# The down matrices' requests, from SP to ACT, in the expert stage of a two-layer encoder

## What is computed

```python
DEPTH = 2; D_MODEL = 1024; N_EXPERTS = 32; TOP_K = 2; EXPERT_FF = 512
for i in range(DEPTH):
    ...                                     # conv, attention, gates, cross attention
    h = h + hier_moe(rmsnorm(h, norm_ffn_g[i]), ..., w1[i], w3[i], w2[i])

# inside hier_moe, for the tokens xb of expert e
hdn = jax.nn.silu(xb @ w1[e]) * (xb @ w3[e])      # up: 1024x512, twice
y = hdn @ w2[e]                                   # down: 512x1024
out = jnp.einsum('nkd,nk->nd', y, weights)
```

## Time and profile before

| | us |
|---|---|
| median of the runs | 1767.76 |
| lowest and highest of the runs | 1762.47 and 1770.13 |
| span of the profiled execution | 1763.5 |
| PE busy | 1498.1 (85%) |
| DVE busy | 616.6 (35%) |
| ACT busy | 528.7 (30%) |
| POOL busy | 57.3 (3%) |
| bytes moved by DMA | 530.92 MB, mean 301 GB/s |

### The profile page before, as it was taken

One profiled execution on the slowest core, in us unless ns is written; L12 is line 12 of the kernel. 1 busy time (PEld: TensorE's weight loads), 2 busy tenths in 40 slices (PEclk: granted clock), 3 DMA queues, 4 the chain that ended last, 5 costly groups with the idle time before them and its releaser, 6 DMA issues.

```text
span 1763.5 us, 24557 instructions
## 1 busy us (share of the span) xinstructions
PE 1498.1 (85%) x9704; PEld 1006.0 (57%) x9704; DVE 616.6 (35%) x1020; ACT 528.7 (30%) x829; POOL 57.3 (3%) x100
## 2 busy tenths in 40 slices
PE   8999999999886767676789999999998777776766
PEld 7788889886332323232277888998853232323322
DVE  5556777554110100000054668775530000000101
ACT  5436564543100000000153465645431000000001
POOL 3011000000000000000000200000000000000000
PEclk8999999999998888889899999999999989898988
DMA  8536335755999999999955462457469999999997
GB/s 232 191 120 215 127 113 191 286 191 217 405 422 422 422 421 422 422 422 422 415 181 187 126 203 97 144 193 285 162 280 423 422 422 422 422 422 422 422 422 306
DMA packets 118165, 530.92 MB, mean 301 GB/s; under 512 B 8808, under 2 KB 9000, under 8 KB 68934
## 3 DMA queue, kind: packets, MB, share of 16 engines
q1 hardware_dynamic: 114944, 524.13, 74.9%
q0 software_dynamic: 3136, 5.73, 1.6%
q10 hardware_dynamic: 12, 0.05, 0.0%
HBM read 524.63 MB, written 1.05 MB: 298 GB/s over the span
## 4 chain that ended last, share of the span: by engine, by line
PE 56%; DMA 36%; DVE 2%; SPq 2%; issue 2%; ACT 2%; PEldq 0%; DVEq 0%; ACTq 0%
DMA ring<-in_w_dram 35%; PE ps L2054 11%; PE ps L1670 7%; PE ps L1675 7%; PE ps L1671 7%; PE ps L1726 4%; PE ps L1727 4%; PE ps L1732 4%; SPq L561 2%; PE ps L1772 2%; PE ps L1695 1%; PE ps L1701 1%; PE ps L1696 1%; PE ps L1829 1%; PE ps L2023 1%
## 5 line engine op out<-in xcount | busy, mean ns | idle before, releaser
L2054 PE MATMUL ps<-ring,big 128*32 128x512 f32 x2048 | 297.9, 736 | 207.1 <-DMA ring<-in_w_dram 205.4
L1132 DVE TENSOR_TENSOR weight_split<-ring,weight_split 128x1024 fp32r<-128x1024 f32 x224 | 270.7, 1222 | 164.9 <-ACT weight_split L734 162.9
L2054 PEld LDWEIGHTS ps<-ring,big 128*32 128x32 f32 x2048 | 83.1, 131 | 417.2 <-issue 417.1
L734 ACT ACTIVATE weight_split<-ring 128x1024 fp32r<-128x1024 f32 x224 | 234.5, 1058 | 214.9 <-PE ps L1732 82.7
L1531 DVE TENSOR_TENSOR big<-big,ps 128x256 f32<-128x256 f32 x32 | 13.5, 421 | 697.0 <-ACT big L1021 697.0
L1670 PE MATMUL ps<-operand_split,weight_split 128*128 128x256 f32 x896 | 228.5, 293 | 4.9 <-issue 3.8
L1671 PE MATMUL ps<-operand_split,weight_split 128*128 128x256 f32 x896 | 220.5, 283 | 0.0
L1670 PEld LDWEIGHTS ps<-operand_split,weight_split 128*128 128x128 f32 x896 | 171.9, 192 | 18.5 <-issue 17.4
L1017 ACT ACTIVATE big<-ps 128x512 f32<-128x512 f32 x32 | 33.6, 1049 | 474.7 <-PE ps L2054 474.7
L1671 PEld LDWEIGHTS ps<-operand_split,weight_split 128*128 128x128 f32 x896 | 172.3, 192 | 2.0 <-issue 1.9
L2023 PEld LDWEIGHTS ps<-big 128*128 128x128 f32 x1024 | 119.1, 192 | 43.7 <-issue 42.2
(11 more groups left out here) (249 smaller groups left out, 1531.4 us busy)
## 6 DMA issues: line engine op xcount, KB each, us to landing
ring<-in_w_dram SPq DMA_DIRECT2D x376, 1024.0 KB, 17.9
ring<-in_w_in_dram SPq DMA_DIRECT2D x28, 2048.0 KB, 8.1
ring<-in_w_xkv_dram SPq DMA_DIRECT2D x8, 2048.0 KB, 8.1
ring<-in_w_attn_out_dram SPq DMA_DIRECT2D x4, 2048.0 KB, 8.4
ring<-in_w_conv_out_dram SPq DMA_DIRECT2D x4, 2048.0 KB, 8.0
ring<-in_w_out_dram SPq DMA_DIRECT2D x4, 2048.0 KB, 8.4
big<-in_w_dram SPq DMA_DIRECT2D x8, 1024.0 KB, 13.1
ring<-in_w_xq_dram SPq DMA_DIRECT2D x4, 2048.0 KB, 8.3
```

The costliest lines, as they stand in the source:

```text
L734: act.activation(split_quarter(k, 0), landed_quarter(k), ACT.Copy).then_inc(w_hi, 1)
L1132: dve.tensor_tensor(split_quarter(k, 1), landed_quarter(k), split_quarter(k, 0).bitcast(F32), ALU.subtract).then_inc(w_lo, 1)
L2054: last = pe.matmul(ps[CAP * j:CAP * (j + 1), 1, :], xe[:, k, e * CAP:(e + 1) * CAP], pair_slot(j)[:, k, :], start=(k == 0), stop=(k == DC ...
```

## The change

The four requests for the down matrices of a pair leave SP's program, except in the first pair of a layer, and enter ACT's `next_scatter_columns`, behind ACT's wait for both `added` and ahead of its scatter copies. SP's two waits for the down matmuls of the pair before go with them. The same bytes go to the same places, and the same semaphores `down_in` are counted; the requests now go to ACT's queue.

```diff
+        def down_half_source(L, e, k):
+            return w2[L, e].rearrange("(p c) n -> p c n", p=P)[:, 2 * k:2 * k + 2, :]
...
-                for k in range(2):
+                for k in range(2 if first else 0):
                     for e in range(2):
                         if k == 0:
                             left(False, 2 + e)
-                        sp.dma_start(down_slot(4 + e)[:, 2 * k:2 * k + 2, :],
-                                     w2[L, 2 * i + e].rearrange("(p c) n -> p c n", p=P)[:, 2 * k:2 * k + 2, :]
+                        sp.dma_start(down_slot(4 + e)[:, 2 * k:2 * k + 2, :], down_half_source(L, 2 * i + e, k)
                                      ).then_inc(down_in[k][e], 16)
...
-                def next_scatter_columns():
+                def next_scatter_columns(i):
                     n = act.snap(u)
                     for s in range(TT):
                         act.wait_ge(added[s], n)
+                    for k in range(2):
+                        for e in range(2):
+                            act.dma_start(down_slot(4 + e)[:, 2 * k:2 * k + 2, :], down_half_source(L, 2 * i + e, k)
+                                          ).then_inc(down_in[k][e], 16)
                     scatter_columns(n)
...
-                with act.Fori(1, PAIRS) as _i:
-                    next_scatter_columns()
+                with act.Fori(1, PAIRS) as i:
+                    next_scatter_columns(i)
                     hidden()
```

More of the change, by code:

```diff
@@ L1036, in _ @@
                     with act.Fori(1, passes) as _p:
-                        with act.Fori(0, PAIRS) as _i:
-                            next_scatter_columns()
+                        with act.Fori(0, PAIRS) as i:
+                            next_scatter_columns(i)
                             hidden()
```

## The result

| | before | after |
|---|---|---|
| median of the runs, us | 1766.24 | 1782.83 |
| lowest to highest | 1762.47 to 1770.13 | 1779.33 to 1785.35 |
| span of the profiled execution | 1763.5 | 1780.8 |

There are four runs of each; the three of before that gave the median of 1767.76 above are among them. The change makes the kernel slower, by under 1%: ratio 1.0087, 95% interval 1.0063 to 1.0111, 16.6 us between the medians. A second series of the same kernel gave 1.0072 (1.0051 to 1.0092), 13.9 us. The forecast was +17.1 us, a span of 1780.6 and a time of 1784.9.

The account below looks back on a forecast made before the run. DMA engines were taken to bound the expert stages. Per layer, 4.5 us of late stream start plus 4.5 of byte order, less small savings, gave 8.4 + 8.7 = 17.1 us on the 1767.76 median: 1784.9 us, range 1772 to 1804.

Parts of the forecast that it names:

- The bound: Expert stages of both layers: DMA engines bound them; only idle DMA time or more PE work after the last byte lengthens them.
- SP's and ACT's instructions: Expert pairs: SP loses four requests and two waits, ACT gains four requests, about 1.9 us; effect on the time 0.
- The late start: Start of each layer's expert stage: pair 1's downs are requested only after the adds, so the stream starts 4.5 us later.
- S to U15: From pair 0's ups starting (S) to the last pair's second up halves starting (U15); predicted 9.0 us later per layer.
- Equal turns: Expert stages: SP's and ACT's queues alternate on the DMA engines, so steady pairs still average 29.84 us; chance 0.70.
- The single line: Rival for the queues: ACT's requests stand behind SP's, only the delayed beginning counts, 9 us, 1776.8 us; chance 0.10.
- unequal turns: Rival in steady pairs: one queue is favoured; 1809 us with two of three packets for ACT; chance 0.11, including lower rate.
- a higher rate: Rival in shared stretches: two busy queues pull more; at 460 GB/s 1758 us; chance 0.09, of which 0.05 faster.
- The recurrence: Steady pairs: next r is 12.15 - r, steps 17.7 + 2r; alternating 31.1 and 28.6 us, average unchanged at 29.84 us.
- r: Stream time of a pair's downs left at its last up byte; 6.7 at pair 2, 5.45 at pair 15, harmless between 4.2 and 7.95.
- end term: End of each layer's expert stage: last ups complete 5.45 us ahead of the stream's end instead of 9.95; 4.5 us.
- The end: Stage ends: U15 of layer 0 at 879.1, next slab 893.8 instead of 885.42; 8.4 us late, layer 1 8.7 us.

Follow-up runs that it names:

- experiment 2: The change, but ACT asks for the downs as early as SP did, waiting only for the previous pair's down matmuls; 1790.6 us, 1.0133 of the kernel before.
- experiment 4: The change, but SP asks for the downs of each layer's second pair (pair 1) at the old time; 1771.12 us, 1.0024 of the kernel before.
- experiment 5: The change, but SP asks for the downs of pairs 1 and 15 of each layer, ACT for pairs 2 to 14; 1767.64 us, 1.0005 of before.
- experiment 3: The change, but SP asks for the downs of each layer's last pair (15), behind its ups; 1775.14 us, 1.0052 of the kernel before.
- experiment 1: The kernel before, all down requests on SP in the old order, but each waiting for the previous pair's adds; 1773.0 us, 1.0039 of before.

## Why the prediction was right, and where not

**The bound.** Right: the slices inside the stages are at 421 to 423 GB/s in all kernels but two, experiment 2 (down to 409, where the engines idle) and a single slice of experiment 4 (417). Only idle DMA time and PE's work behind the last ups count. Experiment 5 shows it: 26 pairs changed, and the time stayed.

**SP's and ACT's instructions.** Right at 0. ACT's four requests took 1.85 us (I had taken 1.9) and 2.20 in pair 1; the scatter copies end long before PE's transposes.

**The late start.** Right in place and size. Predicted 4.5 us a layer; the request came 4.6 us later in the stage, and the stream lost 4.7 and 4.5 us. Alone it cost 4.7 and 4.1 us from S to U15 (experiment 3); the 3.9 and 3.0 of experiment 1 belong to a request that was only 2.7 us later. One name was wrong: the 1.7 us "from request to first byte" are the delay to an equal start at full rate. Windows of half a microsecond have the first packets between 449.0 and 449.5, at 213 GB/s, about 1 us behind the request of 448.20, and over 400 GB/s only from 451. The sum used it rightly.

**Equal turns.** Right, and the least certain step: it rested on one window with POOL. The trace of experiment 2 has 289 packets to 288, at a total of 419 GB/s. The single line as a rival is out (the number of PE's waits at the up matmuls alone would settle it, 28 and not 54), and so are unequal turns and a higher rate.

**The recurrence.** r' = 12.15 - r and the steps 17.7 + 2r give an alternation of 31.1 and 28.6 us. Layer 0 swung wider, between about 26.1 and 33.5; the step of 32.6 from pair 2 to pair 3 (488.85 to 521.46) means r = 7.45 where I had 6.7. Layer 1 swung less and not regularly, between 28.3 and 31.7; what damped it there is open. That the average stays near the period of before is what mattered, and it did. The end term hangs on the last r: 9.95 - r. I had r = 5.45 and 4.5 us for both layers. The downs left behind the last ups give r = 4.8 and 7.3, so 5.1 and 2.6 us. This is the term that was mis-sized: for S to U15 I had 9.0 in both layers, and layer 0 came out 0.5 above it, layer 1 1.9 below. In the second profile the same term is 5.8 and 5.0. So r at the last pair came out between 4.15 and 7.3 in the four stages: across the range that I had given it (4.2 to 7.95), and not at the one value that the sum took.

**The end.** Predicted: U15 of layer 0 at 879.1 and the slab at 893.8; measured 879.10 and 893.57. Such closeness is luck: S was 0.6 us early, the next slab was asked for 6.4 us after U15 (885.50) and not 5.5, and it then took 8.1 us from request to use where I had added up 9.2. What I had not reckoned with is the 2.3 us between U15 and the end of the adds in layer 0. There the granted clock was 0.50, the level of 1.2 GHz, while the last ups and downs ran:

```profile
882.00:884.00 2.00, 2.00 (x12) 0.45 (x8) 0.00 (x0) 0.00 (x0) 0.00 (x0) 0.50 0.11 45
...
888.00:890.00 2.00, 1.91 (x12) 0.59 (x16) 0.04 (x1) 1.99 (x5) 0.00 (x0) 0.50 1.04 406
```

PE had idled 10.9 us ahead of them; the ups took 6.25 us and the last downs 5.18, against 5.34 and 3.85. I can't call this a cost of the change: in its second profile the same stretch took 15.93 us, less than the 16.42 of before, and experiment 1, whose PE waits are those of before, has 18.73. Nor does it follow the wait of PE ahead of it: 12.1 us of waiting came ahead of the 15.93, and 4.3 and 4.0 us ahead of the 18.92 and 19.16 of experiment 4. What sets it is open.

**The sum.** Late start 4.7 + 4.5 us, end term 5.1 + 2.6, together 16.9 against the 16.6 from S to U15. In the second profile the parts make 20.0 against 19.5. Taken from the medians: experiment 3 has +8.3 for the start, so 5.6 to 8.3 are left of the change's 13.9 to 16.6 for the end; experiment 5, with both undone, is at +1.2. The parts add up within what the intervals allow. That the forecast of 17.1 met the first series to 0.5 us is luck in part: the end of layer 1 was 1.9 us shorter than predicted, and in the spans the dense part of layer 1 was 1.5 shorter and layer 0 had 2.3 behind U15, neither of which I had reckoned with. The second series is 3.2 us under the forecast.

## What to carry to other kernels

In this kernel, in a stage that the DMA engines bound, moving a request cost nothing while the engines had work. In such a stage look at the first transfer of the stage, where they don't, and at the last, behind which the compute engine still has to finish. A second queue was not a second lane here but a different order of bytes: two queues took equal turns, so a transfer that is needed later takes half the rate from the one that is needed first, and asking for it earlier made that worse. When you read an experiment, check in its trace that the edit moved the thing by as much as the change did: the request of experiment 1 was late by 2.7 us, that of the change by 4.6. If requests are already in the order of need on one queue, leave them there; if some must move, leave the first and the last of the stage.

## What the runs showed of the hardware that I had not expected

SP's and ACT's queues shared the 16 engines to one packet in 289 over 10 us (experiment 2, 473 to 483), at a total of 419 GB/s, where one queue alone moved 422: one queue had left nothing over. And if the later-needed transfer is asked for early enough, both queues run dry at the same moment: in experiment 2 the engines idled 4 us, just behind the start of a stage that is bound by them.

The granted clock in the last stretch of a stage differed from one execution to the next of the same kernel: the last ups and downs took 6.25 and 5.18 us in one profile of the change and 5.04 and 3.64 in the other.
